# The last residual turned by VectorE in 32 x 32 blocks and added there, in place of PE's transposes into PSUM

## The reference

```python
def second_block(...):
    ...
    up = causal_depthwise_conv(jnp.einsum("bsd,df->bsf", hn, w_up[l]), ffn_conv_w[l])
    gate, val = jnp.split(up, 2, axis=-1)
    h = h + jnp.einsum("bsf,fd->bsd", jax.nn.silu(gate) * val, w_down[l])
    return rms_norm_2(h, final_norm)      # h * rsqrt(mean(h * h) + 1e-5) * g, per token
```

## Time and profile before

| | us |
|---|---|
| median of 3 runs | 1213.22 (1212.61 to 1214.97) |
| profiled execution | 1213.27 |
| its span, first to last instruction | 1211.5 |
| PE busy | 1203.4 (99%) |
| DVE, ACT, POOL busy | 606.1, 484.0, 548.1 |
| last projection: transposes, then matmuls | 1168.47 to 1171.96, 1171.96 to 1206.57 |

### The profile page before, as it was taken

One profiled execution on the slowest core, in us unless ns is written; L12 is line 12 of the kernel. 1 busy time (PEld: TensorE's weight loads), 2 busy tenths in 40 slices (PEclk: granted clock), 3 DMA queues, 4 the chain that ended last, 5 costly groups with the idle time before them and its releaser, 6 DMA issues.

```text
span 1211.5 us, 16875 instructions
## 1 busy us (share of the span) xinstructions
PE 1203.4 (99%) x5740; PEld 987.5 (82%) x5740; DVE 606.1 (50%) x862; ACT 484.0 (40%) x729; POOL 548.1 (45%) x316
## 2 busy tenths in 40 slices
PE   9999999999999999999999999999999999999998
PEld 7777788888888888888777888888888888888888
DVE  6457765331243214484586355475677146632652
ACT  5454545432232213244565433344554224322444
POOL 4932154444434444464323666554354444443433
PEclk9999999999999999999999999999999999999999
DMA  8531133333333333233221333343233333333221
GB/s 201 157 87 54 35 107 100 92 102 94 97 103 88 105 88 95 72 110 106 86 62 36 96 100 98 108 127 104 70 104 104 104 88 94 96 105 101 77 65 71
DMA packets 220115, 114.77 MB, mean 95 GB/s; under 512 B 4171, under 2 KB 218913, under 8 KB 220065
## 3 DMA queue, kind: packets, MB, share of 16 engines
q1 hardware_dynamic: 219905, 113.83, 32.7%
q10 hardware_dynamic: 160, 0.27, 0.1%
HBM read 111.99 MB, written 2.10 MB: 94 GB/s over the span
## 4 chain that ended last, share of the span: by engine, by line
PE 96%; SPq 1%; DMA 1%; DVE 1%; issue 0%; POOL 0%; ACT 0%; ACTq 0%
PE ps L1342 88%; PE ps L1694 3%; PE ps L1497 1%; PE ps L1487 1%; PE ps L1513 1%; DMA w_stage<-in_w_in 1%; SPq L497 1%; SPq L484 0%; PE ps L1684 0%; PE ps L1550 0%; PE ps L1407 0%; SPq L459 0%; PE ps L1376 0%; POOL w_lo L553 0%; SPq L451 0%
## 5 line engine op out<-in xcount | busy, mean ns | idle before, releaser
L553 POOL TENSOR_TENSOR w_lo<-w_stage,w_hi 128x1024 fp32r<-128x1024 f32 x216 | 526.7, 2445 | 636.4 <-ACT w_hi L641 636.4
L1342 PE MATMUL ps<-h_hi,w_hi 128*128 128x512 f32 x1100 | 433.7, 394 | 0.2
L1342 PE MATMUL ps<-h_hi,w_lo 128*128 128x512 f32 x1100 | 428.6, 390 | 0.0
L1342 PE MATMUL ps<-h_lo,w_hi 128*128 128x512 f32 x1100 | 428.1, 389 | 0.0
L641 ACT ACTIVATE w_hi<-w_stage 128x1024 fp32r<-128x1024 f32 x216 | 226.9, 1058 | 442.0 <-PE ps L1342 429.0
L1342 PEld LDWEIGHTS ps<-h_hi,w_hi 128*128 128x128 f32 x1100 | 206.5, 188 | 48.6 <-issue 5.2
L1342 PEld LDWEIGHTS ps<-h_hi,w_lo 128*128 128x128 f32 x1100 | 206.4, 188 | 43.5
L1342 PEld LDWEIGHTS ps<-h_lo,w_hi 128*128 128x128 f32 x1100 | 206.6, 188 | 42.9 <-issue 1.0
L906 DVE TENSOR_TENSOR mid<-ps,rs 128x512 f32<-128x512 f32 x130 | 88.5, 687 | 222.9 <-PE ps L1342 222.3
L1342 PE MATMUL ps<-g_hi,w_hi 128*128 128x512 f32 x496 | 193.6, 390 | 0.0
L1342 PE MATMUL ps<-g_hi,w_lo 128*128 128x512 f32 x496 | 193.0, 389 | 0.0
(11 more groups left out here) (178 smaller groups left out, 815.0 us busy)
## 6 DMA issues: line engine op xcount, KB each, us to landing
w_stage<-in_w_up SPq DMA_DIRECT2D x66, 512.0 KB, 3.8
w_stage<-in_w_in SPq DMA_DIRECT2D x48, 512.0 KB, 3.9
w_stage<-in_w_down SPq DMA_DIRECT2D x32, 512.0 KB, 3.8
w_stage<-in_w_gate SPq DMA_DIRECT2D x22, 512.0 KB, 3.8
w_stage<-in_w_out SPq DMA_DIRECT2D x16, 512.0 KB, 3.9
w_stage<-in_w_down SPq DMA_DIRECT2D x16, 384.0 KB, 3.3
mid<-in_x SPq DMA_DIRECT2D x4, 512.0 KB, 5.9
w_stage<-in_w_attn_branch SPq DMA_DIRECT2D x8, 256.0 KB, 2.8
```

The source lines that it names most:

```text
L553: pool.tensor_tensor(w_lo[:, s, c], w_stage[:, s, c], low_of(w_hi[:, s, c]), ALU.subtract).then_inc(w_lo_ready, 1)
L1342: ins = pe.matmul(bank(par if banks is None else banks, m), a, b, start=first and i == 0, stop=last and i == 2)
```

## The change

PE's 32 transposes are dropped, and the first matmul of each bank starts the sum afresh. DVE turns the residual instead, after its last work for the network: `turn_y(0, 4)` in 16 instructions of 32 partitions x 512 elements, `turn_y(4, 6)` and `turn_y(6, 8)` in 16 instructions of 32 x 256 each, from `xT` to `y_out` in SBUF. `add_y(part, t)` adds the sums from PSUM to `y_out`, and the squares, gains and outputs read `y_out` and no longer PSUM. The squares are written to `sq`, and each waits for the one before it. DVE's order is written out: two turns, the adds of part 1 for two tiles, the third turn, the adds of part 0, the other two adds of part 1, and later one add of part 2 per tile. PE runs the first five chunks of j = 0, then five of j = 1, and then the sixth chunk of each; it asks for the free banks only at j = 2, and its j = 3 waits for the adds of part 1 in place of the squares. ACT's order is the same.

```diff
--- before.py
+++ after.py
@@ -274,6 +274,8 @@
         f_ready = sem("f_ready")
         gain_landed = sem("gain_landed")
         y_part = [sem(f"y_part{i}") for i in range(3)]
+        y_turned = sem("y_turned")
+        y_added = [sem(f"y_added{i}") for i in range(3)]
         y_squared = [sem(f"y_squared{i}") for i in range(3)]
         y_gained = sem("y_gained")
         y_biased = sem("y_biased")
@@ -868,8 +870,10 @@
 
             def y_squares(part, t):
                 half, c = Y_PARTS[part]
-                act.wait_ge(y_part[part], t + 1)
-                act.activation(y_out[:, t, y_half(half)][:, c], y_bank(t, half)[:, c], ACT.Square,
+                act.wait_ge(y_added[part], t + 1)
+                if t:
+                    act.wait_ge(y_squared[part], t)
+                act.activation(sq[:, half, c], y_out[:, t, y_half(half)][:, c], ACT.Square,
                                scale=float(D) ** -0.5, accum_out=y_sq[:, part, t:t + 1])\
                    .then_inc(y_squared[part], 1)
 
@@ -1310,24 +1314,59 @@
             dve.memset(f_in[:, :, 0:2], 0.0).then_inc(pads_cleared, 1)
             dve.wait_ge(pads_cleared, 3)
             ffn(FFN2, 3, True)
+
+
+
+            def turn_y(k0, k1):
+                for i in range(4):
+                    for j in range(4):
+                        for k in range(k0, k1, 4):
+                            n = min(4, k1 - k)
+                            features = xT[32 * i:32 * i + 32, k * T:(k + n) * T]\
+                                .rearrange("p (k t c) -> p k t c", k=n, c=P)[:, :, :, 32 * j:32 * j + 32]
+                            tokens = y_out[32 * j:32 * j + 32, :, k * P:(k + n) * P]\
+                                .rearrange("p t (k c) -> p k t c", k=n)[:, :, :, 32 * i:32 * i + 32]
+                            ins = dve.transpose(tokens, features)
+                ins.then_inc(y_turned, 1)
+
+            def add_y(part, t):
+                half, c = Y_PARTS[part]
+                dve.wait_ge(y_part[part], t + 1)
+                o = y_out[:, t, y_half(half)][:, c]
+                dve.tensor_tensor(o, o, y_bank(t, half)[:, c], ALU.add).then_inc(y_added[part], 1)
+
+            turn_y(0, 4)
+            turn_y(4, 6)
+            dve.wait_ge(y_turned, 2)
+            for t in range(2):
+                add_y(1, t)
+            turn_y(6, 8)
+            for t in range(NT):
+                add_y(0, t)
+            for t in range(2, NT):
+                add_y(1, t)
+            dve.wait_ge(y_turned, 3)
             dve.wait_ge(gain_landed, 16)
             for t in range(NT):
                 dve.wait_ge(y_squared[0], t + 1)
                 dve.tensor_scalar(y_bias[:, t:t + 1], y_sq[:, 0, t:t + 1], eps[:, 1:2], None,
                                   ALU.add).then_inc(y_biased, 1)
-                dve.tensor_tensor(y_out[:, t, y_half(0)], y_bank(t, 0), gain_row[:, y_half(0)],
+                dve.tensor_tensor(y_out[:, t, y_half(0)], y_out[:, t, y_half(0)], gain_row[:, y_half(0)],
                                   ALU.mult).then_inc(y_gained, 1)
             for t in range(NT):
                 dve.wait_ge(y_squared[1], t + 1)
                 dve.wait_ge(y_biased, t + 1)
                 dve.tensor_tensor(y_bias[:, t:t + 1], y_bias[:, t:t + 1], y_sq[:, 1, t:t + 1],
                                   ALU.add).then_inc(y_biased, 1)
+            add_y(2, 0)
             for t in range(NT):
                 dve.wait_ge(y_rooted, t + 1)
                 dve.reciprocal(rs_col[:, t:t + 1], rms_col[:, t:t + 1]).then_inc(y_inverted, 1)
                 dve.wait_ge(y_inverted, t + 1)
-                dve.scalar_tensor_tensor(y_out[:, t, y_half(1)], y_bank(t, 1), rs_col[:, t:t + 1],
+                dve.scalar_tensor_tensor(y_out[:, t, y_half(1)], y_out[:, t, y_half(1)], rs_col[:, t:t + 1],
                                          gain_row[:, y_half(1)], ALU.mult, ALU.mult).then_inc(y_vec, 1)
+                if t + 1 < NT:
+                    add_y(2, t + 1)
 
 
         @block.tensor
@@ -1678,43 +1717,43 @@
             ffn(FFN2, 3, FC)
 
 
-            def turn_y(t, half):
-                for k in range(4 * half, 4 * half + 4):
-                    c = slice(k % 4 * P, (k % 4 + 1) * P)
-                    pe.matmul(y_bank(t, half)[:, c], xT[:, k * T + t * P:k * T + (t + 1) * P], ident[:, :],
-                              is_transpose=True, start=k == 4 * half, stop=False)
-
-            def y_step(j, t, k, stop):
+            def y_step(j, t, k):
                 o = y_bank(t, j // 2)[:, j % 2 * 256:j % 2 * 256 + 256].rearrange("p (m c) -> p m c", m=2)
                 x_hi, x_lo = (g[:, k * T + t * P:k * T + (t + 1) * P] for g in (g_hi, g_lo))
                 wh, wl = (w[:, (LAST + j) % 2, :].rearrange("p (m k c) -> p m k c", m=2, c=P)[:, :, k, :]
                           for w in (w_hi, w_lo))
                 for i, (a, b) in enumerate(((x_hi, wh), (x_hi, wl), (x_lo, wh))):
-
-                    ins = pe.matmul(o, a, b, start=False, stop=stop and i == 2, skip_group_check=j == 3)
+                    ins = pe.matmul(o, a, b, start=j != 1 and k == 0 and i == 0,
+                                    stop=j > 0 and k == NF - 1 and i == 2)
                 return ins
 
             NF = GROUPS[-1][1]
             F_DONE = FC + GROUPS[-1][0]
-            for t in range(NT):
-                turn_y(t, 0)
-            for t in (2, 3, 0, 1):
-                pe.wait_ge(evacuated, 2 * LAST - (2 if t >= 2 else 0))
-                turn_y(t, 1)
-            pe.wait_ge(w_lo_ready, 2 * LAST + 2)
-            for k in range(NF):
-                pe.wait_ge(f_ready, F_DONE + k + 1)
+
+            for j in range(2):
+                pe.wait_ge(w_lo_ready, 2 * (LAST + j) + 2)
+                for k in range(NF - 1):
+                    pe.wait_ge(f_ready, F_DONE + k + 1)
+                    for t in range(NT):
+                        y_step(j, t, k)
+            pe.wait_ge(f_ready, F_DONE + NF)
+            for j in range(2):
                 for t in range(NT):
-                    ins = y_step(0, t, k, False)
-            ins.then_inc(mm_done, 2)
-            for j in range(1, D // 256):
+                    ins = y_step(j, t, NF - 1)
+                    if j == 1:
+                        ins.then_inc(y_part[0], 1)
+                if j == 0:
+                    ins.then_inc(mm_done, 2)
+            for j in range(2, D // 256):
                 pe.wait_ge(w_lo_ready, 2 * (LAST + j) + 2)
                 for t in range(NT):
-                    if j == 3:
-
-                        pe.wait_ge(y_squared[1], t + 1)
+                    if j == 2:
+                        pe.wait_ge(evacuated, 2 * LAST - (2 if t >= 2 else 0))
+                    else:
+
+                        pe.wait_ge(y_added[1], t + 1)
                     for k in range(NF):
-                        ins = y_step(j, t, k, j > 0 and k == NF - 1)
+                        ins = y_step(j, t, k)
                     ins.then_inc(y_part[j - 1], 1)
```

## The result

The changed kernel takes 1232.5 us (median of 6 runs, 1231.9 to 1234.0) against 1213.5 for the kernel before beside it: a ratio of 1.0157, 95% interval 1.0148 to 1.0167, 1.6% slower. The forecast was 1231.5. The profiled execution has a span of 1230.7, 19.2 more than before.

What follows compares the result with a forecast made beforehand. PE, busy 99%, was taken to bound the kernel. Last panel's start 1213.55 + 8.64 matmuls + 2.1 clock + 4.93 tail + 0.5 add = 1229.7 span; with 1.77 around it, 1231.5 us, range 1224 to 1243.

Steps and rivals of the forecast that it cites:

- The first stall: PE before panel j = 2: idle 4.57 us, from 1185.75 to 1190.32, until the split weights are ready.
- The turns: VectorE's 48 block transposes from 1177.08: one element per cycle, no overlap, 0.74 and 0.47 us each.
- The adds of part 1: VectorE's adds for tiles 0 and 1 after two turns: sums already there, 0.8 us, ending at 1197.2.
- ACT and POOL: Weights of j = 3 queue behind part 0's squares: 1207.45, plus 5.91 us of high and low parts, plus 0.2.
- The second stall: PE before panel j = 3: idle 14.6 us, from 1198.96 to 1213.55, waiting for the weights.
- The clock: PE's clock falls in the long wait before j = 3; 4.2 us at half rate, a loss of 2.1.
- The tail: After PE's last matmul: 4.93 us as before plus 0.5 for one add and a handover.
- No queue builds up: Last panel: VectorE and ACT take 2.15 us per tile with the add, while PE gives one every 2.16.
- Rival B: Transposes share a port with POOL, so its low parts for j = 2 delay the chain 4.8 us: 1236.3; 10%.
- Rival C: VectorE's transposes take two cycles per element, 17.1 us more in all: 1248.6; 10%.
- E: PE waits only for j = 2's weights; those of j = 3 are not held up by adds: 1214.9; 4%.
- D: PE does not wait for weights, and the 3.49 us of dropped transposes are won: 1210.3; 5%.

## Why the prediction was right

It held in its mechanism, and each term but a few lay within some tenths; the total was off by 1.0 us. Part of that closeness is luck, since misses in both directions cancel: the turns were shorter, the wait for tile 1, the squares and POOL's low parts longer. The changed profile lies 0.3 us later than the one before already at the start of this part (VectorE's last product at 1176.70 against 1176.39).

- **The first stall**: 4.57 us forecast, ending 1190.32; measured 4.50 and 1190.51. The reading that the gain is gone at the third panel already was right in the order of events. But this stall costs the run next to nothing, as the run with PE's order of before shows, by 1.0 us.
- **The turns**: forecast 11.8 and 7.5 for 16 of each kind; measured 11.45 and 7.17 (0.716 and 0.448 each, of which 0.702 and 0.436 are the instruction itself). One element per cycle and no overlap were right; the gap behind a turn is 0.01 to 0.02 and not the 0.05 of the clears. All 48 together are 1.0 us shorter than forecast.
- **The adds of part 1**: expected not to wait. The second waited 0.70 for tile 1, because the clock had fallen in the first stall. I had allowed 0 to 0.3 for that; with shorter turns it came to the same end (1197.5 against 1197.2).
- **ACT and POOL**: the high parts at 1207.63 (forecast 1207.45). The forecast let VectorE's third add decide and the square of tile 2 begin 0.05 behind it. That add ends at 1206.55, the square begins at 1207.01: the change makes each square wait for the one before it, and so they start 0.82 apart (1205.38, 1206.19, 1207.01) where the adds start 0.61 apart. In the kernel before, two squares with no such wait between them start 0.57 apart (1191.18 and 1191.75). POOL's share of the collision with VectorE's products was mis-sized: 0.2 forecast, 0.68 measured (5.45 against 4.77 before). In the run with ACT's order altered, where no product runs beside them, four low parts take 9.34, 4.67 a pair.
- **The second stall** began later than forecast (1201.4, again the clock) and so was 12.9 and not 14.6; what counts is its end, 1214.25 against 1213.55.
- **The clock**: a loss of 2.1 in the last panel forecast, 2.3 measured (10.95 against 8.64). That it takes as long to come back as to fall was a guess, and it came back after 4.7 us. That 4.2 came so near is luck: in the other runs the way back from a stall took 3.0 to 6.0 us (last section). Whether the first stall would bring the fall the forecast left open; it did, and cost PE 2.3 in the third panel as well, hidden behind VectorE's chain.
- **The tail**: 5.43 forecast, 5.5 measured. "No queue builds up" was not quite so: VectorE's last adds of part 2 come 2.19 apart (1220.93, 1223.12, 1225.31), a little more than PE's 2.16.
- **Rival B** (a port shared with POOL) is shown wrong: none of the 48 turns took more than 0.708 us, though POOL's low parts ran from 1185.8 to 1190.5 among them, and these took 4.65 where 4.77 stood before. **Rival C** (two cycles per element) too. What E describes, the stall for the third panel's weights without the one for the last panel's, came about in two experiments, VectorE's adds first and ACT's order. They took 1224.9 and 1224.3 and not E's 1214.9: its price left out that VectorE, with all its turns behind the last product, comes to its first add of part 2 only at 1211.27 and 1210.60. D's price, 1210.3, was right for a kernel that has no stall at all: the one with every order altered and the turns early took 1210.1.

Where the 19 us lie depends on the sequence in which they are taken away. Starting from the changed kernel: 8.0 for the length of the turns, 6.0 for ACT's order, 6.8 for PE's, 1.6 for VectorE's, 22.4 in all, which leads to 3.2 us below the kernel before. PE's 3.49 of transposes less 0.5 of longer tail would be 3.0.

## What to carry to other kernels

When work moves off the bounding engine, follow the signals that this engine sends: merging two panels here moved the signal "buffer read" from 8.64 us before the next use to 1.44, and a weight split of 6 us no longer fitted. Work given to an engine with idle time is free only in the gaps where it idles; put behind its last product it became the longest chain, while in the gaps of the loop it cost nothing that the time shows (1210.1 measured, 1210.3 by the transposes and the tail alone). And an in-order queue passes a delay on to whatever stands behind the waiting instruction: the weights had nothing to do with the residual, but stood behind its squares.

## What the runs showed of the hardware

- A stall's length does not tell when the clock falls, nor how soon it comes back. In the changed kernel it fell about 2.2 us into the first stall and 3.9 into the second; before, 4.2 after the end of work. With VectorE's adds first, the same first stall (4.52) brought the fall only after 4.1 us: the window 1189 to 1190 reads 0.96, 1190 to 1192 reads 0.50. There it was back 3.0 us after the next matmul (1192 to 1194 reads 0.67); in the changed kernel that took 4.5 and 4.7, and with the early turns and ACT's order 6.0 (PE starts at 1191.06, 1191 to 1197 reads 0.50 and 1197 to 1198 reads 0.96). The run with ACT's order altered stood for only 1.81 us, and the clock fell when PE was already at work again: its matmuls follow at 0.12, 0.16 and then 0.22 us from 1207.5 on, and the window 1206 to 1208 reads 0.84. The run with PE's order of before stood for 1.52 and stayed at 1.00.
- Two SBUF operands on VectorE beside POOL's low parts cost both: VectorE's products took 2.72 and 2.70 us in place of 0.68, and POOL's pair 0.68 more. The Trainium skill ("SBUF — State Buffer", the practical consequences of its port table) says that such an instruction contends with a GpSimd instruction that reads SBUF; the trace agrees, and the turns, with one operand each, show the other half of that rule (none over 0.708 beside POOL, POOL's pair 4.65).
